# Three weight buffers instead of two, the low part written over the raw copy, and a second, casting load for the high part

## The reference, cut to what matters

```python
for l in range(2):
    h = rmsnorm(x, norm_w[l])
    proj = h @ w_in[l]                 # 2048 x 6160
    ...                                # ssd, convolution, attention
    x = x + y @ w_out[l]               # 2048 x 2048
u = rmsnorm_2(h, g_pre)
z = u @ w_in_2                         # 2048 x 9216
...                                    # banded attention, recurrence
h = h + rmsnorm_2(y @ w_out_2, g_post)
gate = sigmoid(h @ w_pg)               # 2048 x 2048
e = p_l @ w_pp
h = h + rmsnorm_2(gate * e, g_ple)
```

## Time and profile before

| what | value |
|---|---|
| median of 3 runs | 3073.88 us (3073.58 to 3075.14) |
| the profiled execution | 3075.18 us, its span 3073.9 us |
| mean granted TensorE clock | 0.991 |
| TensorE matmuls busy | 2975.6 us, 97% |
| GpSimd busy | 2019.9 us, 66% |
| VectorE busy | 1766.3 us, 57% |
| weight loads (`w_raw`) | 240 transfers, 234 MB in all, 4.9 us from issue to landing for one of 1 MB |

### The profile page before, as it was taken

How to read it: one execution, slowest core, us unless ns; L and a number is a source line. 1 busy time by engine, 2 the same in 40 slices (tenths; PEclk the granted TensorE clock), 3 DMA queues, 4 the chain that set the end, 5 groups by cost and what they waited for, 6 DMA issues and landing times.

```text
span 3073.9 us, 39316 instructions
## 1 busy us (share of the span) xinstructions
PE 2975.6 (97%) x15124; PEld 2347.5 (76%) x15124; DVE 1766.3 (57%) x2344; ACT 974.4 (32%) x1683; POOL 2019.9 (66%) x1897
## 2 busy tenths in 40 slices
PE   8999999999999999999999899999999999899997
PEld 6887877788778878777887677777777777688886
DVE  8645887751474569776317433333778887910612
ACT  5343123320234331333103223223444444511411
POOL 7666676576676657755757655555676777567766
PEclk9999999999999999999999999999999999999999
DMA  4322222243223222222432222222222122142222
GB/s 156 124 98 95 96 89 79 80 142 128 102 100 110 103 78 94 91 81 76 174 123 98 76 80 72 84 72 80 71 77 81 69 83 83 56 158 96 98 95 96
DMA packets 56939, 295.51 MB, mean 96 GB/s; under 512 B 6544, under 2 KB 6928, under 8 KB 26928
## 3 DMA queue, kind: packets, MB, share of 16 engines
q1 hardware_dynamic: 37856, 253.77, 23.4%
q10 hardware_dynamic: 18896, 39.22, 3.8%
HBM read 275.08 MB, written 12.65 MB: 94 GB/s over the span
## 4 chain that ended last, share of the span: by engine, by line
PE 74%; DVE 15%; ACT 4%; POOL 3%; issue 2%; DMA 1%; ACTq 1%; DVEq 0%; SPq 0%; POOLq 0%
PE bank L439 60%; PE bank L963 6%; POOL w_lo L2619 2%; DVE rec_ex L2435 1%; DVE rec_cum L2300 1%; PE bank L773 1%; POOL w_hi L2617 1%; ACT att_sc L1321 1%; PE bank L782 1%; PE bank L790 1%; PE bank L955 1%; DMA w_raw<-in_wall 1%; DVE att_sc L2176 1%; DVE bank L1902 1%; DVE rec_lk L2427 1%
## 5 line engine op out<-in xcount | busy, mean ns | idle before, releaser
L439 PE MATMUL bank<-h_hi,w_lo 128*128 128x512 f32 x3456 | 1396.2, 404 | 30.9 <-POOL w_lo L2619 28.7
L2619 POOL TENSOR_TENSOR w_lo<-w_raw,w_hi 128x512 fp32r<-128x512 f32 x936 | 1306.6, 1396 | 78.0
L439 PE MATMUL bank<-h_hi,w_hi 128*128 128x512 f32 x3456 | 1354.8, 392 | 0.0
L439 PE MATMUL bank<-h_lo,w_hi 128*128 128x512 f32 x3456 | 1352.8, 391 | 0.0
L2617 POOL TENSOR_SCALAR w_hi<-w_raw 128x512 fp32r<-128x512 f32 x936 | 716.4, 765 | 964.8 <-PE bank L439 828.1
L439 PEld LDWEIGHTS bank<-h_hi,w_lo 128*128 128x128 f32 x3456 | 653.7, 189 | 225.0 <-issue 60.4
L439 PEld LDWEIGHTS bank<-h_hi,w_hi 128*128 128x128 f32 x3456 | 652.7, 189 | 140.7
L439 PEld LDWEIGHTS bank<-h_lo,w_hi 128*128 128x128 f32 x3456 | 654.3, 189 | 135.8 <-issue 8.4
L1024 ACT ACTIVATE raw<-bank 128x512 f32<-128x512 f32 x148 | 88.6, 599 | 406.3 <-PE bank L439 367.3
L2101 DVE SCALAR_TENSOR_TENSOR bank<-cfm_up,par,bank 128x512 f32<-128x512 f32 x232 | 175.4, 756 | 8.3
L2262 DVE TENSOR_TENSOR xT<-bank,xT 128x512 f32<-128x512 f32 x32 | 22.1, 692 | 218.1 <-PE bank L439 217.4
(11 more groups left out here) (376 smaller groups left out, 2977.9 us busy)
## 6 DMA issues: line engine op xcount, KB each, us to landing
w_raw<-in_wall SPq DMA_DIRECT2D x232, 1024.0 KB, 4.9
ssd_abc<-acs_scratch ACTq DMA_DIRECT2D x16, 512.0 KB, 3.7
x_scratch<-xT ACTq DMA_DIRECT2D x8, 1024.0 KB, 4.5
xT<-x_scratch ACTq DMA_DIRECT2D x8, 1024.0 KB, 8.9
xT<-in_x ACTq DMA_DIRECT2D x4, 1024.0 KB, 9.5
xT<-in_x SPq DMA_DIRECT2D x3, 1024.0 KB, 11.0
out<-last_z SPq DMA_DIRECT2D x4, 768.0 KB, 3.3
w_raw<-in_wall SPq DMA_DIRECT2D x8, 256.0 KB, 9.5
```

The costliest lines, as they stand in the source:

```text
L439: mm = t.matmul(bank[BANK[u]][:, :], w[:, CS16[k]], h[:, k, :], start=(k == 0 and w is m.w_lo[b]), stop=(k == KT - 1 and w is m.w_hi[b] an ...
L2619: g.tensor_tensor(m.w_lo[b][:, part], m.w_raw[b][:, part], m.w_hi[b][:, part].bitcast(F32), ALU.subtract).then_inc(*s.lo.inc(u, n))
```

## The change

Sets of buffers become three (unit u uses set u % 3) of two buffers each: `w_raw` and `w_lo` now lie at the same addresses, so the subtraction writes over the raw weights it reads. The memory used is the same (six buffers of 8 KB).

For most units the TENSOR_SCALAR on GpSimd goes. Instead GpSimd's queue issues a second transfer of the same 1 MB from `wall` straight into `w_hi`, which converts float32 to float32r on the way. GpSimd issues it for unit u+1 after the last subtraction of unit u and after TensorE has finished unit u-2, and then waits for both the raw load and the casting load of u+1 before it subtracts. SyncE's raw load of unit u now waits until TensorE has finished unit u-3 (before: until GpSimd had finished u-2).

Units 0 and 1, and five units that are the second of a pair at a stage's start (3, 65, 67, 129, 131; `QUARTERED`), keep the old rounding on GpSimd and are loaded in four pieces, each as TensorE has read the same piece of unit u-3. The piecewise overwriting and the alternation of GpSimd between the units of a pair are gone.

The core of the diff (left out: the same `u % 2` to `u % NW` in `product` and `gate_part`, and the new argument `io`):

```diff
--- before.py
+++ after.py
@@ -98,7 +98,8 @@
         self.hi, self.lo = signal("hi"), signal("lo")
         self.piece = [[signal(f"piece{b}{n}", 16) for n in range(PIECES)] for b in range(2)]
         self.half = [signal(f"half{n}", 16) for n in "qk"]
-        self.raw = [signal(f"raw{b}", 16) for b in range(2)]
+        self.raw = [signal(f"raw{b}", 16) for b in range(NW)]
+        self.cast = [signal(f"cast{b}", 16) for b in range(NW)]
         self.con, self.con1, self.par, self.wd, self.pos, self.p = (signal(n, 16) for n in ("con", "con1", "par", "wd", "pos", "p"))
         self.gple, self.pool = signal("gple", 16), signal("pool")
         self.par2 = signal("par2", 16)
@@ -174,10 +175,8 @@
 
 
 BANK, LAST = _banks()
-PAIRS = [(names[n], names[n + 1]) for names in FIRST.values() for n in (0, 2)]
-PAIRS += [(("wo", l, KT - 2), ("wo", l, KT - 1)) for l in range(DEPTH)]
-PAIRED = frozenset(UNIT[pair[0]] for pair in PAIRS)
-OUT_PAIR = {UNIT["wo", l, 0]: l for l in range(DEPTH + 1)}
+NW = 3
+QUARTERED = frozenset(UNIT[names[n]] for names in FIRST.values() for n in (1, 3)) - {UNIT[FIRST[0][1]]}
 HALVES = (64, 32, 16, 8, 4, 2, 1, 0)
 MARGIN = SSD_K - 1
 X_PARTS = ((0, 1), (1, 2), (2, 4), (4, 8), (8, 12), (12, 16))
@@ -229,9 +228,11 @@
         self.xT = big("xT", [P, KT, T])
         self.y = self.xT
         self.h_hi, self.h_lo = big("h_hi", [P, KT, T], F32R), big("h_lo", [P, KT, T], F32R)
-        self.w_raw = [big(f"w_raw{b}", [P, KT * P]) for b in range(2)]
-        self.w_hi = [big(f"w_hi{b}", [P, KT * P], F32R) for b in range(2)]
-        self.w_lo = [big(f"w_lo{b}", [P, KT * P], F32R) for b in range(2)]
+        self.w_hi = [big(f"w_hi{b}", [P, KT * P], F32R) for b in range(NW)]
+        raws = self.at
+        self.w_raw = [big(f"w_raw{b}", [P, KT * P]) for b in range(NW)]
+        self.at = raws
+        self.w_lo = [big(f"w_lo{b}", [P, KT * P], F32R) for b in range(NW)]
         self.con = big("con", [P, NCON])
         self.ident, self.ones, self.tri = (cols(self.con, CON, n, P) for n in ("ident", "ones", "tri"))
         self.pick = cols(self.con, CON, "pick", SSD_H)
@@ -431,7 +432,7 @@
             t.wait_ge(*(dve if LAST[u] in BY_DVE else act).at("evac", LAST[u]))
 
     def tiles(u, lo, hi):
-        b = u % 2
+        b = u % NW
         for k in range(lo, hi):
             if k % (KT // PIECES) == 0:
                 t.wait_ge(*s.lo.at(u, k // (KT // PIECES)))
...
@@ -2609,36 +2610,42 @@
     last()
 
 
-def pool_engine(nc, m, s):
+def pool_engine(nc, io, m, s):
     g = nc.gpsimd
 
-    def split(u, n):
-        b, part = u % 2, slice(n * PIECE, (n + 1) * PIECE)
+    def rounded(u, n):
+        b, part = u % NW, slice(n * PIECE, (n + 1) * PIECE)
         g.tensor_scalar(m.w_hi[b][:, part], m.w_raw[b][:, part], 1.0, 1.0, ALU.mult, ALU.mult).then_inc(*s.hi.inc(u, n))
         g.wait_ge(*s.hi.at(u, n))
+
+    def rest(u, n):
+        b, part = u % NW, slice(n * PIECE, (n + 1) * PIECE)
         g.tensor_tensor(m.w_lo[b][:, part], m.w_raw[b][:, part], m.w_hi[b][:, part].bitcast(F32), ALU.subtract).then_inc(
             *s.lo.inc(u, n))
 
+    def cast(u):
+        if u < N_UNITS and u not in QUARTERED:
+            if u >= NW:
+                g.wait_ge(*s.unit.at(u - NW))
+            g.dma_start(m.w_hi[u % NW][:, :], io["wall"][u, :, :]).then_inc(*s.cast[u % NW].inc(u))
+
     for n in range(PIECES):
         for u in range(2):
-            g.wait_ge(*s.piece[u][n].at("w"))
-            split(u, n)
-    u = 2
-    while u < N_UNITS:
-        behind_pair = u - 2 in PAIRED or u - 2 in OUT_PAIR
-        us = (u, u + 1) if u in PAIRED or behind_pair else (u,)
-        for b in us:
-            g.wait_ge(*s.raw[b % 2].at(b))
+            g.wait_ge(*s.piece[u][n].at(u))
+            rounded(u, n)
+            rest(u, n)
+    cast(2)
+    for u in range(2, N_UNITS):
+        if u not in QUARTERED:
+            g.wait_ge(*s.raw[u % NW].at(u))
+            g.wait_ge(*s.cast[u % NW].at(u))
         for n in range(PIECES):
-            if behind_pair and n < PIECES - 1:
-                g.wait_ge(*s.pe.at("piece", u - 2, n))
-            elif u - 1 in OUT_PAIR and n < PIECES - 1:
-                g.wait_ge(*s.pe.at("read", OUT_PAIR[u - 1], n))
-            elif n == 0 or behind_pair or u - 1 in OUT_PAIR:
-                g.wait_ge(*s.unit.at(us[-1] - 2))
-            for b in us:
-                split(b, n)
-        u += len(us)
+            if u in QUARTERED:
+                g.wait_ge(*s.piece[1][n].at(u))
+                rounded(u, n)
+            rest(u, n)
+            if n == PIECES - 1:
+                cast(u + 1)
     q, n = m.last, NC - 1
 
     def add(c):
@@ -2672,7 +2679,7 @@
     def pieces(n):
         for u in range(2):
             at = slice(n * PIECE, (n + 1) * PIECE)
-            nc.sync.dma_start(m.w_raw[u][:, at], io["wall"][u, :, at]).then_inc(*s.piece[u][n].inc("w"))
+            nc.sync.dma_start(m.w_raw[u][:, at], io["wall"][u, :, at]).then_inc(*s.piece[u][n].inc(u))
 
     x_part(0)
     pieces(0)
@@ -2684,9 +2691,16 @@
     x_part(5)
     pieces(3)
     for u in range(2, N_UNITS):
-        b = u % 2
-        nc.sync.wait_ge(*s.lo.at(u - 2, PIECES - 1))
-        nc.sync.dma_start(m.w_raw[b][:, :], io["wall"][u, :, :]).then_inc(*s.raw[b].inc(u))
+        b = u % NW
+        if u in QUARTERED:
+            for n in range(PIECES):
+                at = slice(n * PIECE, (n + 1) * PIECE)
+                nc.sync.wait_ge(*(s.pe.at("piece", u - NW, n) if n < PIECES - 1 else s.unit.at(u - NW)))
+                nc.sync.dma_start(m.w_raw[b][:, at], io["wall"][u, :, at]).then_inc(*s.piece[1][n].inc(u))
+        else:
+            if u >= NW:
+                nc.sync.wait_ge(*s.unit.at(u - NW))
+            nc.sync.dma_start(m.w_raw[b][:, :], io["wall"][u, :, :]).then_inc(*s.raw[b].inc(u))
     for c in range(NC):
         nc.sync.wait_ge(*s.dve.at("final", c))
         nc.sync.dma_start(io["out"][CS[c], 0:3 * T], flat(m.last.z[:, 4 * c:4 * c + 3, :])).then_inc(*s.out[0].inc(c))
```

More of the change, by code:

```diff
@@ L953, in product @@
                 at = slice((2 * (n % 2) + k) * T, (2 * (n % 2) + k) * T + T)
-                for h, w in ((q.phi, m.w_lo[u % 2]), (q.plo, m.w_hi[u % 2]), (q.phi, m.w_hi[u % 2])):
-                    mm = t.matmul(ps[:, :], h[:, k, CS[c]], w[:, at], start=(k == 0 and w is m.w_lo[u % 2]),
-                                  stop=(k == 1 and h is q.phi and w is m.w_hi[u % 2]))
+                for h, w in ((q.phi, m.w_lo[u % NW]), (q.plo, m.w_hi[u % NW]), (q.phi, m.w_hi[u % NW])):
+                    mm = t.matmul(ps[:, :], h[:, k, CS[c]], w[:, at], start=(k == 0 and w is m.w_lo[u % NW]),
+                                  stop=(k == 1 and h is q.phi and w is m.w_hi[u % NW]))
             mm.then_inc(*(s.unit.inc(u) if j % 8 == 7 else pe.inc("e", j)))
@@ L961, in gate_part @@
             at = slice(r * T, r * T + T)
-            for h, w in ((m.h_hi, m.w_lo[u % 2]), (m.h_lo, m.w_hi[u % 2]), (m.h_hi, m.w_hi[u % 2])):
-                mm = t.matmul(bank[GATE_BANK[c]][:, :], h[:, k, CS[c]], w[:, at], start=(k == 0 and w is m.w_lo[u % 2]),
-                              stop=(k == KT - 1 and h is m.h_hi and w is m.w_hi[u % 2]))
+            for h, w in ((m.h_hi, m.w_lo[u % NW]), (m.h_lo, m.w_hi[u % NW]), (m.h_hi, m.w_hi[u % NW])):
+                mm = t.matmul(bank[GATE_BANK[c]][:, :], h[:, k, CS[c]], w[:, at], start=(k == 0 and w is m.w_lo[u % NW]),
+                              stop=(k == KT - 1 and h is m.h_hi and w is m.w_hi[u % NW]))
             if c == NC - 1 and r == 3:
@@ L2702, in build @@
         sync_engine(nc, io, m, s)
-        pool_engine(nc, m, s)
+        pool_engine(nc, io, m, s)
         tensor_engine(nc, m, s)
```

## The result

The changed kernel takes 3110.22 us (median of 4 runs, 3107.86 to 3118.82), the kernel before beside it 3074.51 us: ratio 1.0121, 95% interval 1.0104 to 1.0138. The forecast was 3060 us. The time lies in the range, but on the other side of no change.

What follows compares the result with a forecast made beforehand. TensorE was taken as the bound, with a matmul running 97% of the span. From 3073.9 us, -20.5 - 5.2 + 2 + 13.6 - 4 = -14.1 us gave a span of 3059.8, forecast 3060 us, range 3043 to 3195.

Steps and rivals of the forecast that it cites:

- step 7: Raw and casting loads on the DMA engines, dense stretches: they rarely meet, 0 us, up to 6 us.
- step 4: Output products: delay behind the first pair stays, hidden at ordinary units; 6.8 us wait at pairs 62/63 and 126/127, +13.6 us.
- step 6: Whole kernel: GpSimd busy some 690 us less without roundings, so VectorE gains: -4 us, between 0 and 17.
- L: Time from issue to landing of the casting load on GpSimd's queue: 5.7 us taken; no gain at 6.2 us.
- Waits that go: TensorE's waits on GpSimd's `w_lo` at ordinary units, all but the start's 8.2 us, vanish: -20.5 us.
- Clock and what is late next: Half clock returns at 76 to 84 and 1688 to 1713 us, -5.2 us; VectorE's `h_lo` limits around 1700 us, +2 us.
- The pairs at a stage's start: Units 3, 65, 67, 129, 131: piecewise loads and GpSimd's rounding remain beside TensorE's work, costing nothing.
- S: GpSimd's four subtractions of one unit, in series with the casting load: 5.3 us.
- long casting load: Rival, chance 0.40: GpSimd's loop L + S outlasts TensorE's unit; 3085 to 3095 us at L = 6.5, 3201 at 7.9.

Runs made afterwards that it cites:

- early_spaced: Changed kernel with the next casting load issued after the first of four subtractions and GpSimd waiting on its own semaphore after each subtraction: 3068.38 us, ratio 0.9984.
- mixed: Units 0 to 131 as in buffers_timed, from unit 132 on as in early_spaced: 3050.46 us, ratio 0.9932.
- buffers_alone: Changed kernel without the casting load: three sets of buffers, low part written in place, GpSimd rounds all pieces itself: 3090.43 us, ratio 1.0063.
- buffers_timed: buffers_alone, but GpSimd begins a unit only when TensorE has finished unit u-2, except in or just behind pairs: 3057.56 us, ratio 0.9946.
- early_issue: Changed kernel with the next unit's casting load issued after the first of the four subtractions instead of the fourth: 3150.45 us, ratio 1.0256.
- quarter_raw: Changed kernel with three quarters of each raw load left out for units not loaded in pieces, low parts there zero: 3056.14 us, one run.

## Why the prediction was wrong, step by step

Three numbers failed: step 7 (the two loads rarely meet: 0 us), step 4 (the first casting load behind a pair as short as any other, so 6.8 us a product and no wait before the last pair), and step 6 (VectorE's gain of 4 us). The first two are one mistake, L taken without the kernel's own traffic.

1. *Waits that go*: right for the waits that were there; new ones at ordinary units are under 7. No wait on `w_lo` is left at 76, 893, 1645 and 1668 us; at 1720 to 1755 us (unit 132) the trace has only this one:

```profile
PE bank L440 <- DVE h_lo L1821: 1.7, 1, 1.7
```

2 and 3. *Clock and what is late next*: right around 1700 us, also in size. At 76 to 84 us the clock does come back, but TensorE then arrives early at the wait on `raw` at 99 us and is at half clock behind it (0.66 over 10 us, 3.4 us lost), so the 1.7 us were not kept. The stretch up to unit 132 was to gain 8.8 + 3.5 - 2 = 10.3 us, and the lag falls by 10.3 at unit 132; `h_lo` takes the place of `w_lo` as foreseen.

4. *The pairs of the output products*: the delay is there and shows at the last pair, as forecast, but it is longer from its start (see 7). The wait at the last pair is

```profile
831.95 0.79 PE L440 MATMUL bank<-h_hi,w_lo 128*128 128x512 f32 x1 [8.78 <-POOL w_lo L2623]
```

8.8 us, and 8.7 at the second one, for the 6.8 forecast.

5. *The pairs at a stage's start*: right, no wait there.

7. *Both loads at once*: this is the first step that failed; it put them at 0. It said that the casting load of a dense stretch goes out 10 us after the raw one and so rarely meets it. But TensorE frees a set every 10.9 us, so 10 us behind the raw load of unit u the raw load of unit u+1 goes out: by the prediction's own numbers (10.3 growing to 11.4 us) the two meet at nearly every unit. L alone was better than forecast (5.0 to 5.3 us for 5.7), and so was S (5.0 for 5.3); 102 of 227 casting loads shared the engines with most of a raw load, and the median L was 6.7.

In the output products three things made the turns longer, and all three are other traffic. Step 4 gave the first casting load behind the pair L + S = 11.0 us. Its L alone was 11.3 us in the first product and 10.7 in the second, so the load of 52 goes out 16.3 us after its raw load (15.4 for unit 116) and not 10.3. With 5.2 us of load and 1.3 for the first piece that is 22.8 us, and the 21.8 us that hide it are used up from the start. Of the eleven casting loads behind it (units 52 to 62) six took 5.0 to 5.4 us, two that met a raw load 7.0 and 7.4, and the three that also met ACT's stores of x, at units 53, 57 and 61, 8.7, 8.1 and 8.7. So a turn became 11.6 us on average, and TensorE waited at just these units: 1.9 us at 51, then 2.3, 1.9 and 1.6 at 53, 57 and 61, in all 7.6 us between 690 and 823 us, where step 4 had nothing. Each such wait also puts off the next raw load, which SyncE issues when TensorE is done. With an undisturbed L the turn is 5.2 + 5.0 = 10.2 us and the distance shrinks again by 0.7 us a unit. These waits and what they cost in clock are in the two windows (us, busy us of PE, PEld, DVE, ACT, POOL, granted clock, DMA share, GB/s):

```profile
692.00:823.00 131.00, 123.40 (x534) 100.67 (x532) 15.65 (x23) 6.62 (x11) 63.61 (x58) 0.99 0.63 216
823.00:856.00 33.00, 24.22 (x98) 19.74 (x98) 18.70 (x16) 10.76 (x15) 22.50 (x18) 0.84 0.36 121
```

The pair's stretch has a granted 0.84 against 0.88 in the earlier trace rows: 33 x 0.16 = 5.3 us lost to half clock where it was 3.5. Step 4's "the clock falls there as it does now" was too kind. In all, the first two output products cost 28.6 us; steps 1 and 4 made it 2 x (6.8 - 3.2) = 7.2. This is the mechanism of the rival "long casting load", priced there at L = 6.5 with 3085 to 3095; it came through the other loads, not through software or conversion. early_spaced, which takes the load out of the series, waits 1.2 to 1.7 us at units 51, 115 and 203 and at no other unit behind 4. The Trainium skill (DMA: Bandwidth & Descriptors, Issuing engines are not separate DMA queues) says that transfers run on the same 16 engines and interleave, whoever issues them; the 5.0, 7.0 and 8.7 us agree. The 6.15 us of engine time that the Trainium skill (DMA: Bandwidth & Descriptors, Bandwidth) lists for 1 MB from GpSimd isn't seen: here the whole load takes 5.0.

6. *VectorE's gain*: failed in its sign. -4 us was taken; TensorE's waits on ACT and VectorE grew by 12.6 us, 11.3 of it on ACT; the wait on ACT's `raw` at 99 us leads back to VectorE, as shown above. In the recurrence the gain is real (7.3 us of lag, 11 in mixed). But VectorE has lost in the attention stages. (GpSimd itself is busy 1464 us and not 1340: the 227 issues of the casting load count 130.) "GpSimd is busy less, so VectorE gains" looked at a sum. buffers_alone and buffers_timed differ only in when GpSimd works, and by 33 us. early_issue and early_spaced differ only in whether GpSimd pauses, and by 82. In the changed kernel the two readings above show it at work, at 441 and at 76 us: a run of four subtractions falls on instructions of the chain that TensorE waits for next. Between units 4 and 7 all kernels with three sets lose 5.9 to 10.1 us except quarter_raw (1.2), and it is also the only one of them in which VectorE's instructions of 76 to 84 us take 7.5 us, as before, and not 9.6 to 10.2. How much of the rest of the attention stages is of this kind is open: a pause after each subtraction gave back half of the loss in the first one and nothing in the second.

## What to carry over

When a transfer is issued and awaited by the engine that works on its data, its latency is in series with the work, and what counts is its latency under the kernel's own traffic, not alone. When you say that two periodic transfers rarely meet, compare their distance with the period: 10 us behind one raw load was just when the next went out. And a loop that is shorter than its consumer's ends up waiting for the consumer's own event, together with whatever else waits for it; so ask for its length in the collision. And before counting the busy time taken from GpSimd as a gain for VectorE, look at when GpSimd's instructions run and whether they leave gaps: moving them was worth 33 us here and one pause 82, against the 36 us that the change cost.

## What the runs showed of the hardware

- A load of 1 MB with conversion from float32 to float32r, issued from GpSimd, lands after 5.0 to 5.3 us when alone; a plain one from SyncE has a median of 4.9. The issue keeps GpSimd busy for 0.57 us.
- Three subtractions of GpSimd without a pause behind a load's issue held one two-input VectorE instruction for all three (0.69 us became 3.46; the most in the run was 4.1 us over the undisturbed time). A wait of 0.1 us on its own semaphore between them limits this to 1.7 us. The Trainium skill (SBUF — State Buffer, SBUF: two separate sides) has the lock last for an instruction; here it outlasted instructions. That four subtractions without a wait in the changed kernel, which follow a wait for a load's landing, don't do this (1.15 us at most) was not explained.
